# One-pass MLA scores, units by token tile and a folded sample tile in a two-layer encoder step

## Chip, core and metric

The kernel runs on one core of a Trainium2 chip. The metric is the time of one execution on the device in microseconds, as the median of several runs; lower is better.

## The reference, cut to what matters

The kernel computes two layers for a prompt of 512 frames and for 32 new frames of a stream with 128 cached frames ("sample"). All values are fp32, the model width is 1024.

```python
# layer 1, stick-breaking: 16 heads of 64
h = rms_norm(x, g_pre_a)
q, k, v, gate = split(h @ w_in_a, 4);  q, k = rms_norm(q), rms_norm(k)
w = where(mask, exp(log_sigmoid(z) + after), 0)     # after: sums of log_sigmoid(-z) of later keys
x = x + (silu(gate) * (w @ v)) @ w_o_a
# shared latent (512) and rotary key (64) of every frame
latent, kpe = rms_norm(a[:, :512]), rope(rms_norm(a[:, 512:]))      # a = rms_norm(x) @ w_kv_a
k_nope, v = split(latent @ w_kv_b);  k_nope = rms_norm(k_nope)
# layer 2, MLA: 8 heads, 128 + 64 query columns, 128 value columns
qa, gate = split(rms_norm(x) @ w_in_b);  q = rms_norm(qa) @ w_q_b   # then norms and rope
s = (q_nope @ k_nope.T + q_pe @ kpe.T) * 192 ** -0.5
x = x + (silu(gate) * (softmax(where(mask, s, -1e30)) @ v)) @ w_o_b
y = rms_norm(x, g_final)
```

The mask of the prompt is causal, in the MLA layer by chunks of 64 frames.

## The kernel before

**Tiles.** The prompt is four token tiles of 128 (`NT` = 4), the sample a fifth of 32 rows (`TT` = 5), and the cached MLA keys a sixth chunk (`LT` = 6). `TOK` is 544.

**High and low parts.** Large products are not made as fp32 matmuls. ACT copies a value to its high part in a one-pass type (fp32r), DVE or POOL subtracts to get the low part, and TensorE adds three products: high x high, high x low, low x high (`three`, lines 428 to 430). Weights come by SP's DMA queue in pieces of a group into `raw`; ACT makes `whi` (line 1125) and POOL `wlo` (line 1506). A piece is a step "W". Attention scores and value products are true fp32 matmuls, which the profile shows as two records each.

**Orders written out by hand.** Each stage runs steps over pairs of heads. In a step the attention of pair p is mixed with the projections of pair p + 1. A list gives the order, and every engine walks the same list and does its own part of each entry: `STEP_A` and `LAST_A` in the stick-breaking layer (8 pairs), `FILL_D`, `STEP_D` and `LAST_D` in the MLA layer (4 pairs). All queues run in order. Letters of `STEP_A`: C projection chunk of a token tile, G gate, X and Z turns of queries and keys, S scores of a unit, T turn of its weights, O value product. Letters of the MLA lists: Q and K projection chunks (Q queries, K keys and values of two heads), N norm of a chunk, X and Y the turns of a chunk by TensorE into the bank `XB` with ACT's copy to `q2t` or `k2t`, P the last such turn of the pair, S scores of a unit with DVE's maximum (line 1999) and ACT's exponential (line 1429), R its scaling by DVE (line 2007), T the turn of the weights with ACT's copy `wt2`, O the value product and gate. In `LAST_D` H is the split of one head's gated result, E and F are k-steps of the first two of ten output products (`last_product`).

**A chunk in the MLA layer.** TensorE makes it, ACT squares it (and copies the values of a K chunk), DVE sums and forms the mean, POOL raises it to -1/2 (line 1663), DVE makes the norm (and the rotation of a Q chunk), TensorE turns it, ACT copies it.

**A unit** is one head and one query tile against its 1 to 4 key tiles; unit 0 is the sample of both heads. In the MLA layer units go head by head, and a head has one value product over all tiles in the bank `OUT` (line 1023), so O has three parts: sample and two heads.

**Sample tile.** Its stationary operand is 128 columns wide like the others, of which 32 are the sample; the rest of the output rows is not used. It costs three products like the others.

The main MLA list before begins:

```python
STEP_D = [("Q", 0), ("P", 5), ("N", 0), ("K", 0), ("S", 0), ("N", 1), ("R", 0), ("Q", 1), ("X", 0), ("S", 1),
          ("N", 2), ("Y", 0), ("R", 1), ("T", 0), ("K", 1), ("S", 2), ("N", 3), ("W", 0), ("R", 2), ("O", 0),
          ("T", 1), ("Q", 2), ("S", 3), ("X", 1), ("N", 4), ("R", 3), ("K", 2), ("Y", 1), ("Q", 3), ("T", 2),
```

## Time and profile before

| what | value |
|---|---|
| median of 3 runs | 852.7 us (851.94 to 853.42) |
| the profiled execution, its own time | 846.55 us |
| its span, first to last instruction | 844.7 us |
| granted TensorE clock, mean | 0.991 |
| TensorE matmuls busy | 800.8 us, 95% of the span |
| DVE, ACT, POOL busy | 451.9, 331.0, 314.6 us |

The profile is of one execution, which took 6.2 us less than the median of the runs. Durations below come from it. A matmul's record is longer than its share of the engine, since matmuls overlap; the distance from start to start is what it costs. PE is TensorE, PEld its weight loads, DVE VectorE, ACT ScalarE, POOL GpSimd. The stages are: start and first projections to 60 us, eight stick-breaking steps to 394, output product and residual to 460, latent and query projections and gates to 570, the MLA fill to 602, three MLA steps to 759, the last one to 792, output products to 838, tail.

### The profile page before, as it was taken

The numbers are of one execution on the slowest core, as the hardware profiler recorded it, in microseconds if no ns is written. First come the engines' busy times: TensorE is split into PE (matmuls) and PEld (weight loads), VectorE is DVE, ScalarE is ACT, GpSimd is POOL, SyncE is SP. The second block draws the span as 40 slices with busy tenths as digits, with TensorE's granted clock in tenths as the row PEclk, the third lists the DMA queues.
The fourth block names the chain that finished last, engine by engine and source line by source line (L and its number), as shares of the span: only waits on it lengthen the run. The fifth ranks groups of instructions, "written<-read, shape, count | busy, mean of one in ns | idle before, by whom it ended". The sixth has DMA issues, their size and how long they took to land.

```text
span 844.7 us, 13543 instructions
## 1 busy us (share of the span) xinstructions
PE 800.8 (95%) x4623; PEld 654.1 (77%) x4623; DVE 451.9 (53%) x1023; ACT 331.0 (39%) x840; POOL 314.6 (37%) x261
## 2 busy tenths in 40 slices
PE   5799999999999999988999899999999999999996
PEld 4688888878887878756878878998777777765785
DVE  5556666666767585874146432116755555656222
ACT  6444334333333333442177332324444343446211
POOL 5345252534344343551313453445433233333100
PEclk9899999999999999999999999999999999999999
DMA  7631303030303030313223142321102011020211
GB/s 212 159 102 47 87 29 106 26 109 25 107 25 107 25 107 25 101 47 113 79 87 111 69 146 75 88 88 45 44 23 66 1 41 59 26 96 5 106 50 57
DMA packets 68082, 61.68 MB, mean 73 GB/s; under 512 B 7144, under 2 KB 55040, under 8 KB 68032
## 3 DMA queue, kind: packets, MB, share of 16 engines
q1 hardware_dynamic: 68032, 61.04, 23.6%
q8 instruction: 29, 0.48, 0.3%
q14 instruction: 21, 0.17, 0.1%
HBM read 50.85 MB, written 10.17 MB: 72 GB/s over the span
## 4 chain that ended last, share of the span: by engine, by line
PE 87%; DVE 5%; ACT 3%; SPq 1%; issue 1%; POOL 1%; DMA 1%; POOLq 0%; ACTq 0%; DVEq 0%
PE bank L428 17%; PE bank L430 16%; PE bank L429 16%; PE bank L688 5%; PE bank L722 3%; PE bank L995 3%; PE bank L700 3%; PE bank L1039 2%; PE bank L1041 2%; PE bank L1040 2%; PE bank L1023 2%; PE bank L993 2%; PE bank L758 2%; PE bank L760 2%; PE bank L759 2%; PE bank L972 1%
## 5 line engine op out<-in xcount | busy, mean ns | idle before, releaser
L1506 POOL TENSOR_TENSOR wlo<-raw,whi 128x1024 fp32r<-128x1024 f32 (+3 forms) x80 | 194.8, 2443 | 116.8 <-ACT whi L1125 116.5
L428 PE MATMUL bank<-whi,hthi 128*128 128x384 f32 (+1 forms) x360 | 129.5, 360 | 2.5 <-DVE wlo L1717 2.3
L430 PE MATMUL bank<-whi,htlo 128*128 128x384 f32 (+1 forms) x360 | 126.1, 350 | 0.0
L429 PE MATMUL bank<-wlo,hthi 128*128 128x384 f32 (+1 forms) x360 | 126.0, 350 | 0.0
L1125 ACT ACTIVATE whi<-raw 128x1024 fp32r<-128x1024 f32 (+3 forms) x84 | 82.4, 1007 | 24.8 <-PE bank L760 20.6
L1780 DVE TENSOR_TENSOR_SCAN left<-stay 128x512 f32<-128x512 f32 (+4 forms) x72 | 70.8, 983 | 18.8 <-ACT stay L1217 18.5
L1569 POOL TENSOR_TENSOR rstd<-msq,neg_half 128x4 f32<-128x4 f32 x40 | 40.3, 1007 | 98.4 <-DVE msq L1747 97.6
L428 PE MATMUL bank<-hthi,whi 128*128 128x272 f32 x256 | 75.0, 293 | 0.0
L428 PEld LDWEIGHTS bank<-whi,hthi 128*128 128x128 f32 x360 | 69.7, 194 | 6.6 <-issue 5.1
L430 PE MATMUL bank<-hthi,wlo 128*128 128x272 f32 x256 | 73.6, 287 | 0.0
L429 PE MATMUL bank<-htlo,whi 128*128 128x272 f32 x256 | 73.4, 287 | 0.0
L1663 POOL TENSOR_TENSOR rstd<-msq,neg_half 128x2 f32<-128x2 f32 (+1 forms) x44 | 36.8, 837 | 97.7 <-DVE msq L1946 97.3
L430 PEld LDWEIGHTS bank<-whi,htlo 128*128 128x128 f32 x360 | 69.4, 193 | 1.7
L429 PEld LDWEIGHTS bank<-wlo,hthi 128*128 128x128 f32 x360 | 69.5, 193 | 1.5
L1785 DVE TENSOR_TENSOR wgt<-left 128x512 f32<-128x512 f32 (+4 forms) x72 | 66.1, 918 | 3.0
L1182 ACT ACTIVATE sq<-bank 128x256 f32<-128x256 f32 x40 | 15.4, 386 | 112.2 <-PE bank L430 112.2
L688 PE MATMUL bank<-qkt 64*128 64x512 f32 (+3 forms) x128 | 51.4, 482 | 0.0
L429 PEld LDWEIGHTS bank<-htlo,whi 128*128 128x128 f32 x256 | 48.3, 189 | 0.0
L428 PEld LDWEIGHTS bank<-hthi,whi 128*128 128x128 f32 x256 | 48.3, 188 | 0.0
L430 PEld LDWEIGHTS bank<-hthi,wlo 128*128 128x128 f32 x256 | 48.2, 188 | 0.0
L1574 POOL TENSOR_TENSOR gtlo<-gated,gthi 128x544 f32 (+1 forms) x8 | 10.8, 1355 | 94.0 <-ACT gthi L1244 94.0
L1217 ACT ACTIVATE stay<-bank 128x512 f32<-128x512 f32 (+4 forms) x72 | 30.2, 420 | 30.5 <-PE bank L690 29.4
(202 smaller groups left out, 1749.4 us busy)
## 6 DMA issues: line engine op xcount, KB each, us to landing
raw<-in_w_in_a SPq DMA_DIRECT2D x64, 256.0 KB, 3.1
raw<-in_w_in_b SPq DMA_DIRECT2D x24, 256.0 KB, 3.2
raw<-in_w_o_a SPq DMA_DIRECT2D x16, 256.0 KB, 2.8
raw<-in_w_kv_b SPq DMA_DIRECT2D x16, 256.0 KB, 3.1
raw<-in_w_o_b SPq DMA_DIRECT2D x16, 256.0 KB, 3.1
raw<-in_w_q_b SPq DMA_DIRECT2D x16, 192.0 KB, 2.4
x_in<-in_x_prompt SPq DMA_DIRECT2D x4, 512.0 KB, 5.2
out<-qkn SPq DMA_DIRECT2D x8, 256.0 KB, 2.4
```

The source lines that it names most:

```text
L428: eng.matmul(dst, st[0], mv[0], start=(k == 0), stop=False)
L429: eng.matmul(dst, st[0], mv[1], start=False, stop=False)
L430: mm = eng.matmul(dst, st[1], mv[0], start=False, stop=(k == n - 1))
L688: pe.matmul(b[:, 0:(i + 1) * P], qkt[r, par, 0, i * P:(i + 1) * P], qkt[r, par, 1, 0:(i + 1) * P], start=True, stop=True)
L700: mm = pe.transpose(TRB[ub][:, j * P:(j + 1) * P], wgt[:, ub, j * P:(j + 1) * P], ident[:, :])
L1125: nc.scalar.activation(whi[slot][:, c], raw[:, c], ACT.Copy).then_inc(s_hi, 1)
L1217: nc.scalar.activation(stay[0:r, ub, SEQ - n:SEQ], SCR[ub][0:r, 0:n], ACT.Sigmoid, scale=-1.0).then_inc(s_stay, 1)
L1506: nc.gpsimd.tensor_tensor(wlo[slot][:, c], raw[:, c], whi[slot][:, c].bitcast(F32), ALU.subtract).then_inc(s_lo, 1)
L1569: nc.gpsimd.tensor_tensor(rstd[:, sl, :], msq[:, sl, :], neg_half[:, :], ALU.pow).then_inc(s_rs, 1)
L1663: nc.gpsimd.tensor_tensor(rstd[:, sl, 0:w], msq[:, sl, 0:w], neg_half[:, 0:w], ALU.pow).then_inc(s_rs2, 1)
L1780: v.tensor_tensor_scan(out=left[0:r, ub, SEQ - n:SEQ][:, ::-1], data0=back, data1=back, initial=1.0, op0=ALU.mult, op1=ALU.bypass).then_in ...
L1785: v.tensor_tensor(wgt[0:r, ub, 0:n], left[0:r, ub, SEQ - n + 1:SEQ + 1], left[0:r, ub, SEQ - n:SEQ], ALU.subtract).then_inc(s_wgt, 1)
```

## The change

1. **Scores of the MLA layer.** Queries and keys are split like the projections: `qh`, `ql`, `kh`, `kl`, `kpeh`, `kpel`. The rotary part of a query is stacked: 64 rows of its high part on 64 rows of its low part (`qr`), against the rotary key, which lies in both halves. A prompt unit is then five one-pass products in place of two fp32 ones. Keys are padded to 256 columns. ACT copies a turned Q chunk in two operations, DVE subtracts the low parts from `XB` (three operations for Q, one for K). The next turn waits for them (`s_xlo2`).
2. **Units by token tile.** `UNIT_D` takes both heads of a tile one after the other. A value product is per tile and head, of 128 columns each, so O has five parts. There is one query buffer in place of two.
3. **Orders.** Chunks go K0 K1 Q3 K2 Q2 K3 Q1, sample K and Q, cached K, Q0. `FILL_D`, `STEP_D` and `LAST_D` are rewritten: C is a chunk, V its turn with ACT's copy and DVE's low part.
4. **Folded sample.** The low part of the sample lies in 32 more columns of the high part, so that one stationary operand holds both. Two products in place of three give both halves in different rows, which are added afterwards: in `STEP_A` by a copy of ACT and an addition of DVE (step L), in the two output products by a second addition. POOL fills the columns.
5. **Last products.** Order of tiles 3, 2, 1, 0, sample; three products are begun inside the last step (E, F, B); the last two heads are split tile by tile (J).
6. **Stick-breaking.** The weights are written over `stay`; the tile `wgt` is gone.

```diff
-UNIT_D = [None] + [(h, i) for h in range(2) for i in reversed(range(NT))]
+UNIT_D = [None] + [(h, i) for i in reversed(range(NT)) for h in range(2)]
+CHUNKS = [("K", 0), ("K", 1), ("Q", 3), ("K", 2), ("Q", 2), ("K", 3), ("Q", 1), ("K", NT), ("Q", NT), ("K", TT), ("Q", 0)]
+STEP_D = [("C", 0), ("P", CD - 1), ("S", 0), ("N", 0), ("C", 1), ("R", 0), ("S", 1), ("N", 1), ("V", 0), ("C", 2),
+          ("T", 0), ("R", 1), ("N", 2), ("V", 1), ("S", 2), ("W", 0),
+          ("C", 3), ("O", 0), ("T", 1), ("R", 2), ("N", 3), ("S", 3), ("V", 2), ("C", 4), ("T", 2), ("R", 3), ("N", 4),
+          ("V", 3), ("S", 4), ("O", 1), ("W", 1),
+          ("C", 5), ("T", 3), ("R", 4), ("N", 5), ("S", 5), ("V", 4), ("C", 6), ("T", 4), ("R", 5), ("N", 6), ("V", 5),
+          ("S", 6), ("O", 2), ("W", 2),
+          ("C", 7), ("T", 5), ("R", 6), ("N", 7), ("S", 7), ("V", 6), ("C", 8), ("T", 6), ("R", 7), ("N", 8), ("V", 7),
+          ("S", 8), ("O", 3), ("W", 3),
+          ("C", 9), ("T", 7), ("R", 8), ("N", 9), ("V", 8), ("C", 10), ("T", 8), ("N", 10), ("V", 9), ("O", 4)]
 FILL_D = []
...
+    FILL_D.append(("C", _j))
     if _j:
         FILL_D.append(("N", _j - 1))
     if _j in (2, 4, 6, 8):
         FILL_D.append(("W", (_j - 2) // 2))
     if _j > 2:
-        FILL_D.append((TURN[CHUNKS[_j - 3][0]], CHUNKS[_j - 3][1]))
+        FILL_D.append(("V", _j - 3))
+LAST_D = [("P", CD - 1), ("S", 0), ("H", 0), ("S", 1), ("R", 0), ("H", 1), ("W", 0), ("E", 0), ("T", 0), ("R", 1), ("S", 2),
+          ("H", 2), ("E", 1), ("O", 0), ("T", 1), ("R", 2), ("S", 3), ("W", 1), ("E", 2), ("H", 3), ("T", 2), ("R", 3),
+          ("S", 4), ("E", 3), ("O", 1), ("F", 0), ("H", 4), ("T", 3), ("R", 4), ("S", 5), ("W", 2), ("E", 4), ("H", 5),
...
 # proj_a, TensorE
+                if c == NT:
+                    two(pe, b[:, 0:3 * P], [(acol(ht[0], k, c, HS), w[k]) for k in range(KD)]).then_inc(s_proj, 1)
+                    return
 # turn_qk, TensorE
                 if begun(CD * q + c):
                     pe.wait_ge(s_xev2, CD * q + c)
+                if begun(LD * q + lows(c)):
+                    pe.wait_ge(s_xlo2, LD * q + lows(c))
 # score_d, TensorE
-                pe.matmul(b[:, 0:(i + 1) * P], q2t[:, par, h, i * P:(i + 1) * P], k2t[:, par, h, 0:(i + 1) * P], ...)
-                pe.matmul(b[:, 0:(i + 1) * P], q2t[r, par, 2, i * P:(i + 1) * P], kpet[r, 0:(i + 1) * P], ...)
+                n = max(2, i + 1) * P
+                pe.matmul(dst, qh[:, h, tile], kh[:, par, h, 0:n], start=True, stop=False)
+                pe.matmul(dst, qh[:, h, tile], kl[:, par, h, 0:n], start=False, stop=False)
+                pe.matmul(dst, ql[:, h, tile], kh[:, par, h, 0:n], start=False, stop=False)
+                pe.matmul(dst, qr[:, h, tile], kpeh[:, 0:n], start=False, stop=False)
+                pe.matmul(dst, qr[:, h, tile], kpel[:, 0:n], start=False, stop=True)
 # out_d, TensorE
+                for h in range(2):
+                    for j in range(i + 1):
+                        mm = pe.matmul(OUT[:, c0 + h * P:c0 + (h + 1) * P], v2[:, par, h, j, :], wt2[:, h, j, :], ...)
 # xlo_d, DVE, new
+                if what == "K":
+                    v.tensor_tensor(kl[:, par, :, tile], nope, kh[:, par, :, tile].bitcast(F32), ALU.subtract).then_inc(s_xlo2, 1)
+                    return
+                v.tensor_tensor(ql[:, :, tile], nope, qh[:, :, tile].bitcast(F32), ALU.subtract)
+                for h in range(2):
+                    last = v.tensor_tensor(qr[other, h, tile], XB[own, 2 * P:3 * P], qr[own, h, tile].bitcast(F32), ALU.subtract)
+                last.then_inc(s_xlo2, 1)
```

## Rows read from the trace of the kernel before

**Rows 1.** Page, chain that ended last, share of the span by engine.
```profile
PE 87%; DVE 5%; ACT 3%; SPq 1%; issue 1%; POOL 1%; DMA 1%; POOLq 0%; ACTq 0%; DVEq 0%
```

**Rows 2.** Windows: length, busy PE PEld DVE ACT POOL (records), clock, DMA share, GB/s.
```profile
276.70:319.90 43.20, 42.91 (x282) 35.86 (x282) 28.65 (x45) 16.37 (x41) 17.98 (x10) 1.00 0.21 64
...
570.20:602.02 31.82, 30.34 (x159) 26.41 (x158) 23.09 (x79) 13.05 (x31) 17.83 (x16) 1.00 0.20 59
602.02:654.32 52.30, 51.79 (x255) 38.17 (x255) 28.91 (x110) 22.82 (x61) 17.66 (x15) 1.00 0.13 36
...
758.94:792.36 33.42, 32.21 (x139) 19.38 (x138) 16.94 (x37) 16.63 (x39) 9.72 (x6) 1.00 0.20 75
792.36:838.30 45.94, 45.90 (x198) 36.85 (x197) 11.11 (x14) 5.26 (x9) 2.98 (x8) 1.00 0.10 40
```

**Rows 3.** Timeline of PE in a stick-breaking step: start, us, what.
```profile
283.69 0.34 PE L428 MATMUL bank<-whi,hthi 128*128 128x384 f32 x1
...
291.37 0.34 PE L430 MATMUL bank<-whi,htlo 128*128 128x384 f32 x1
...
308.98 0.29 PE L428 MATMUL bank<-hthi,whi 128*128 128x272 f32 x1
...
311.45 0.28 PE L430 MATMUL bank<-hthi,wlo 128*128 128x272 f32 x1
```

**Rows 4.** Chain in the first MLA step: start, us on the chain, what.
```profile
611.39 0.86 PE bank L993 x2
612.25 1.05 PE bank L995 x2
613.46 0.23 PE bank L972 x2
...
614.14 0.23 PE bank L429
...
618.31 0.33 PE bank L1018 x2
...
629.19 0.22 PE bank L993 x2
629.42 0.41 PE bank L995 x2
...
637.37 2.21 PE bank L1023 x8
```

**Rows 5.** Timeline of DVE in the second MLA step.
```profile
660.48 0.29 DVE L1988 TENSOR_TENSOR qn<-pe_tmp 128x128 f32<-128x128 f32 x1
...
665.69 0.69 DVE L1999 TENSOR_REDUCE neg_max<-bank 128x1 f32<-128x512 f32 x1 [0.93 <-PE bank L997]
...
683.48 0.29 DVE L2007 TENSOR_SCALAR prob<-prob,p_inv 128x128 f32<-128x128 f32 x1
...
689.65 0.61 DVE L1962 SCALAR_TENSOR_TENSOR kn<-bank,rstd,g_kn 128x128 f32<-128x128 f32 x2 [0.81 <-POOL rstd L1663]
...
702.42 0.61 DVE L2007 TENSOR_SCALAR prob<-prob,p_inv 128x128 f32<-128x128 f32 x1
```

**Rows 6.** Timeline of ACT in the second MLA step.
```profile
656.45 0.49 ACT L1398 ACTIVATE sqd<-bank 128x384 f32<-128x384 f32 x1 [4.04 <-PE bank L430]
...
666.42 0.69 ACT L1429 ACTIVATE prob<-bank,neg_max 128x512 f32<-128x512 f32 x1 [2.26 <-DVE neg_max L1999]
...
671.71 0.94 ACT L1125 ACTIVATE whi<-raw 128x896 fp32r<-128x896 f32 x1
...
676.76 0.48 ACT L1414 ACTIVATE q2t<-bank 128x384 f32<-128x384 f32 x1
...
687.73 0.38 ACT L1401 ACTIVATE sqd<-bank 128x256 f32<-128x256 f32 x1 [1.21 <-PE bank L430]
```

**Rows 7.** Timeline of POOL in the fill ahead of the MLA steps.
```profile
579.82 2.12 POOL L1506 TENSOR_TENSOR wlo<-raw,whi 128x896 fp32r<-128x896 f32 x1
```

**Rows 8.** Timeline of DVE before the fill, a gate's product with PSUM.
```profile
564.78 0.44 DVE L1919 TENSOR_TENSOR sg<-bank,sigc 128x272 f32<-128x272 f32 x1 [2.57 <-ACT sigc L1381]
```

More of the change, by code:

```diff
@@ L430, in three, with two @@
                 mm = eng.matmul(dst, st[1], mv[0], start=False, stop=(k == n - 1))
+            return mm
+        def two(eng, dst, pairs):
+            n = len(pairs)
+            for k, (st, mv) in enumerate(pairs):
+                eng.matmul(dst, st, mv[0], start=(k == 0), stop=False)
+                mm = eng.matmul(dst, st, mv[1], start=False, stop=(k == n - 1))
             return mm
@@ L1667, in step_d @@
                 for what, n in order_d(p):
[L1668 to L1669 removed]
+                    if what == "C" and ahead:
+                        rms_d(p + 1, 1 - par, *CHUNKS[n])
                     elif what == "W":
@@ L1955, in norm_d @@
                 dve.wait_ge(s_act2, CD * q + c + 1)
-                before = CD * q + (CHUNK_D[what, t - 2] + 1 if t > 1 else 0)
+                rank = RANK_D[what, t]
+                before = CD * q + max([0] + [CHUNK_D[s] + 1 for s in CHUNKS if s[0] == what and RANK_D[s] == rank - 2])
                 if begun(before):
```

535 lines of the change are left out of this document (333 added, 202 removed), and 18 rows, old and new, of tables (LAST_D, STEP_A, STEP_D).

## The prediction

> **What bounds the kernel now.** I read the chain that ended last first: TensorE carries 87% of it [rows 1]. Then the busy time by stage, to see how full TensorE is where the change works [rows 2]. In a stick-breaking step 42.9 of 43.2 us are busy. The fill ahead of the MLA loop takes 31.8 us, a full MLA step 52.3 (three of them, 602.0 to 758.9), the last step 33.4 and the output products 45.9. Every matmul taken out there gives its whole period back, as long as the others keep up. Whether they do is read from the third view, the timelines of the other engines [rows 5 to 8]: what a chunk or a unit takes from TensorE's result until TensorE can use it again. All queues are in order, so a late piece holds up everything written behind it.
>
> **TensorE's own work.** The price of a high/low matmul comes from starts: 45 of 384 columns begin between 283.69 and 291.37 us, 0.175 us each; 21 of 272 columns between 308.98 and 311.45, 0.124 each [rows 3]; one of 512 takes 0.23 [rows 4].
>
> *Folded sample.* A pair's sample chunk drops from 24 to 16 matmuls: 8 pairs x 8 x 0.175 = -11.2 us. The new ACT copy and DVE add lie behind four other chunks' worth of work before the transposes need them, and DVE is busy 28.7 of 43.2 us [rows 2]; if that cover were gone it would cost about 1 us a pair. In the first output product 8 of 512 columns go in each half, 16 in all, but six of them in the last stick-breaking step, where TensorE waits for DVE anyway; 10 x 0.23 = -2.3. POOL's extra 32 columns there lie on the path: +0.3. The second product loses 16: -3.7.
>
> *Scores.* A 512-key unit costs 0.86 + 1.05 us for its two fp32 products and 0.16 for the mask, 2.07 in all; the 128-key one 0.22 + 0.41 + 0.16 [rows 4]. Five one-pass products cost 5 x 0.23 = 1.15, 5 x 0.175, and 5 x 0.12 for 256 and for 128 keys (padded to 256; 256 columns lie just under the 272-column row). With 0.07 for a mask that no longer follows a 64-row product: 1.22, 0.94, 0.66, 0.66 against 2.07, 1.65, 1.22, 0.80. A head saves 2.26, a pair 4.5, four pairs -18. With the mask's 0.16 kept it is -15.
>
> *Value products.* A head's 4 products, 1280 columns in all, become 10 of 128. They take 2.21 us now [rows 4]. An fp32 matmul of 128 columns takes 0.22 (both records), so 10 take 2.2: nothing. The other bound is the 32-column product of the sample, which took 0.33 for its two records: +1.1 a head, +8.8 in all. I take nothing, since the row of 0.22 has the new shape, 128 columns on 128.
>
> *Edits I cost at nothing.* The sigmoid of unit u in the stick-breaking layer now waits for the turn of unit u-2, and not its scan; TensorE does that turn ahead of the score the sigmoid needs, so the wait is always met. Copies into the single query buffer wait for scores of the tile that stand several entries ahead in STEP_D. SP loads the residual in another order and `g_final` behind it, after the last score, where some 35 us of output products lie ahead of the first norm; without that cover it would be a few us once. The five banks for the last products take away waits that TensorE does not have now (45.9 of 45.9 us busy) [rows 2].
>
> By TensorE alone the sum is -11.2 - 2.0 - 3.7 - 18 = -35 us.
>
> **What the new order does to the others.** This is the part that decides. Three things come together. XB is one bank: chunk c+1 may be turned only when the low part of chunk c is subtracted by DVE (`s_xlo2`), which stands behind ACT's copies. In STEP_D a chunk's norm N now stands ahead of the next unit's S, so DVE takes the maximum only after it. And ACT's weight piece W stands behind that unit's exponential, with POOL's piece ahead of the next chunk's power.
>
> Prices [rows 5 to 8]: a Q chunk from its square to the end of its norm 656.45 to 660.77, 4.3 us; a K chunk 687.73 to 690.26, 2.5, of it 0.8 waiting for POOL and 0.6 norm, so 1.3 once POOL is free; maximum 0.7 for 512 keys, taken as 0.5 and 0.35 for fewer; exponential 0.69 and the read of its sum, 0.8, taken as 0.7 and 0.6 for fewer; ACT's piece 0.94; POOL's piece 2.12. Q evacuation was one 0.48 copy, now two, 0.66. The low part is 0.4 for K (a 272-column operation on PSUM took 0.44) and 0.8 for Q, that plus two 128-column ones.
>
> Walk one step, C0 at 0. Chunks cost 2.75 (K) and 2.1 (Q). C0, turn, S0, C1, S1, turn, C2: chunk 2 (Q) ends at 10.9. Then norm 4.35, low part K 0.4, maximum 0.6, exponential 0.8, ACT piece 0.95, POOL piece 2.15, power and norm of chunk 3 1.3, maximum 0.5, exponential 0.7, Q copies 0.65, low part Q 0.8: about 13 us, until 23.9. TensorE has 10 us of its own work in between (V1, S2, C3, O0, T1, S3, V2, C4, T2: 20.5), and its next turn V3 waits 2.9 with its score, O1 and chunk 5 queued behind. From that low part the loop closes again: sums 0.8, power 1.0, norm 1.65, low 0.4, maximum 0.5, exponential 0.65, pieces 0.9 + 2.15, power and norm 1.3, maximum 0.35, exponential 0.6, copies 0.65, low 0.8 = 11.8, against 9.4 of TensorE's work: V5 waits 2.5. V5 to V7 is 11.2 against 8.5: 2.7. V9 needs chunk 9's norm, 8.7 against 7.1: 1.6. A step has 46.6 us of TensorE's work and takes 56.4; before it had 51 and took 52.3. Three steps: +12.3.
>
> *Fill.* Two chunks, K and Q, are 5.4 us of TensorE's work. DVE and POOL in series take sums 0.85, power 1.0, POOL piece 2.12, Q norm 1.65, Q low part 0.85 = 6.5. Walked from the first chunk, V1, V3, V5, V7 and V9 wait 1.5, 1.3, 1.2, 1.2 and 0.6, 5.8 us in all, where before 1.5 was lost at the end: +4.3.
>
> *Last step and products.* The turn of the last chunk (Q0) is no longer covered by a K chunk: 2.9. E, F and B stand right behind the H that feeds them. H's DVE part stands behind a maximum, and its ACT part behind a weight piece: E0 waits 1, T1 2, E2 1.3, E3 2, the rest 1.5, 7.7 in all. From the step's start to the last product: 2.9 + 33.6 of work + 7.7 + 35.1 of products left = 79.3, the same as 758.94 to 838.28 now. The 8 us saved there are eaten.
>
> The lock of an SBUF port bears on this: a DVE scale of 128 columns took 0.61 us while POOL's piece ran (702.42), against 0.29 for the same operation at 683.48 [rows 5]. The Trainium skill's page "SBUF — State Buffer", section "Who interferes with whom", says that DVE's two-port modes, and DVE operations with two SBUF inputs, wait for a reading POOL operation to end; the trace agrees with the 0.61. By that rule R1 and R3 of the last step wait for the piece (my T1 above, from the row); the low parts, with one input in PSUM, would not.
>
> *Shared latent.* Four low parts of the rotary key go ahead of latl on DVE, 0.2 to 0.5 each, mostly in stretches that wait on DVE: +0.8. *Tail.* The sample tile needs two more half additions, one exposed: +0.7.
>
> **Sum.** -11.2 - 2.0 + 0.8 + 4.3 + 12.3 + 0 + 0.7 = +4.9 us. The profiled execution took 846.55 us (span 844.7 and 1.9 around it), so it would become 851.4. The median of the runs lies 6.2 above it, 852.7, and I put the change on that: about 857.5.
>
> **Rivals.** The first two end on the other side. *The others keep up* (TensorE stays the bound): -35, and +1.5 for latent and tail, 819. Speaks for it: DVE is busy only 29 of 52 us in a step, ACT 22, POOL 18 [rows 2]. Against: those are sums, and the chain above is a wait, not a load. 0.12. *POOL's piece is not in the loop* (ACT reaches its piece earlier, or raw and order let the power go ahead): three waits a step lose 2.1 each, 3 x 6.3 = -19: 838. It decides once the loop is below 10 us. 0.20. *The value products pay for their weight loads* at 0.33 a product: 866; 0.07. *The loops are longer still* (handoffs of 0.1 in twelve links, or R in the way of N): 868; 0.05. The forecast itself, waits as walked, 850 to 865: 0.56.
>
> What a measurement of this kernel tells from no change is 0.2%, 1.7 us. Of the forecast 0.10 lies within it, the rest above. Faster 0.32, within 0.11, slower 0.57. Range: down to 836 to take in the second rival, up to 868 for the value bound; outside are the first rival and a little above.
>
> **What would show it.** Right: about 41.8 us for a stick-breaking step; an MLA step of 54 to 58 with TensorE idle before the transposes of kn at V3, V5 and V7, released by DVE's subtraction from XB; a fill of about 36; POOL's piece starting later after its chunk than now. Wrong: steps near 47 to 50 without such gaps, an L1023 successor over 0.12 us a record, or a sample fold that holds up the transposes of a pair. The forecast fails first where the order of S, N and W on DVE and ACT binds less than I walked it.

## The result, and the profile after

The changed kernel took 896.4 us in the median of four runs, the kernel before 852.3 beside it: a ratio of 1.0505, 95% interval 1.0454 to 1.0555. It is 44 us slower. I had forecast slower, but 857.5 and at most 868.

First the page of the changed kernel: busy time by engine, and the chain that ended last by engine.

```profile
PE 799.3 (90%) x4655; PEld 668.5 (75%) x4655; DVE 485.6 (55%) x1121; ACT 336.5 (38%) x867; POOL 313.9 (35%) x270
...
PE 52%; issue 15%; DVE 15%; POOL 10%; ACT 5%; SPq 1%; DMA 1%; POOLq 0%; DVEq 0%; ACTq 0%
```

TensorE carried 87% of the chain before [rows 1] and carries 52% now. VectorE, POOL and ScalarE together went from 9% to 30%, and "issue", time in which an engine waited for nothing that the profile shows, from 1% to 15%.

Then the stages: a stick-breaking step, the fill, two MLA steps, and the last step with the output products. The columns are those of [rows 2], and the rows answer to them.

```profile
283.57:326.93 43.36, 42.01 (x274) 34.84 (x275) 28.89 (x46) 16.75 (x42) 18.29 (x11) 1.00 0.21 64
577.95:615.90 37.95, 31.15 (x158) 26.02 (x157) 22.90 (x87) 13.73 (x34) 17.82 (x16) 1.00 0.17 49
615.90:676.84 60.94, 53.20 (x286) 44.55 (x286) 36.04 (x125) 23.35 (x65) 16.66 (x14) 0.92 0.11 31
676.84:738.21 61.37, 53.53 (x288) 44.66 (x287) 36.73 (x128) 21.79 (x63) 17.67 (x15) 0.92 0.10 32
800.20:883.40 83.20, 74.43 (x354) 58.98 (x353) 34.39 (x76) 22.61 (x52) 13.87 (x15) 0.96 0.14 53
```

Two things are to be seen. An MLA step leaves TensorE idle for 7.8 of 61.4 us, and its granted clock in that step is 0.92 of full speed, where it was 1.00 [rows 2]. Over the whole span it was 0.959 against 0.991 before. The stages add up as follows (us, from one profiled execution of each; the last column is my sum cut to the same stages).

| stage | before | after | change | forecast |
|---|---|---|---|---|
| start to the first stick-breaking step | 60.3 | 62.7 | +2.4 | -1.4 |
| seven steps | 303.1 | 308.4 | +5.3 | -9.8 |
| last stick-breaking step to the fill | 206.9 | 206.9 | 0 | -1.2 |
| fill | 31.8 | 38.0 | +6.1 | +4.3 |
| three MLA steps | 156.9 | 184.3 | +27.4 | +12.3 |
| last step and output products | 79.3 | 83.1 | +3.8 | 0 |
| tail | 6.4 | 7.2 | +0.8 | +0.7 |
| sum | 844.7 | 890.5 | +45.8 | +4.9 |

**The MLA step.** The waits of TensorE in the second one, grouped by what it waited for, and then the chain across the wait ahead of V3 (start, us on the chain, what).

```profile
PE bank L1049 <- DVE qr L2163: 7.3, 3, 2.9
PE bank L1110 <- ACT wt L1568: 0.3, 1, 0.3
```

```profile
695.90 0.43 DVE ssq L2097
...
696.36 1.47 DVE msq L2100
...
697.89 0.71 POOL rstd L1798
...
698.62 0.61 DVE kn L2117 x2
699.23 0.47 DVE neg_max L2175
...
700.40 0.27 ACT qh L1540
700.67 0.28 ACT qr L1541
...
700.98 0.41 DVE ql L2158
...
702.16 0.63 PE bank L1049 x2
```

This is the loop that I walked, link by link: chunk, mean square, POOL's power, norm, maximum, exponential, copies, low part, turn. The three waits stand at V3, V5 and V7, released by the last subtraction from XB. POOL's piece shows in it twice: the power starts at 697.89, right behind the piece (695.67 to 697.79), and the mean square of 2 columns took 1.47 us while the piece ran, where the next one took 0.17. The maximum, and the exponential behind it, are in this loop because of the new order.

What I did not see coming is behind the wait. Here are the transposes at its end and a score product behind them, and the same product of 512 keys at full clock.

```profile
702.16 0.63 PE L1049 MATMUL bank<-ident,kn 128*128 128x128 f32 x2 [2.92 <-DVE qr L2163]
...
702.90 0.52 PE L1076 MATMUL bank<-kl,qh 128*128 128x384 f32 x1
703.22 0.52 PE L1077 MATMUL bank<-kh,ql 128*128 128x384 f32 x1
...
714.97 0.41 PE L1049 MATMUL bank<-ident,kn 128*128 128x128 f32 x2 [1.49 <-DVE qr L2163]
```

```profile
623.62 0.40 PE L1075 MATMUL bank<-kh,qh 128*128 128x512 f32 x1
623.86 0.40 PE L1076 MATMUL bank<-kl,qh 128*128 128x512 f32 x1
```

At 702.9 a product of 384 columns starts 0.32 us before the next; at 623.6 one of 512 starts 0.24 before it. From 702.2 to 705.6 the granted clock is at its lower level, 1.2 GHz (0.5), and again from 726.1 to 732.9, at V7's wait. Each of the three MLA steps of this trace has 10.2 us at 1.2 GHz, and each such stretch begins near the end of an idle one of 2.9 us (from 1.3 us ahead of its end to 0.1 behind it). The kernel before had none in its MLA layer.

**The stick-breaking step.** The folded sample chunk takes 2.98 us in place of 4.36, as forecast. But the step takes 43.2 to 44.2 us at full clock, not 41.8, and one of the seven, with 6.8 us at 1.2 GHz, takes 46.2. TensorE's waits over the seven steps:

```profile
PE bank L770 <- DVE stay L1925: 7.9, 10, 1.1
...
```

These are the turns T2 (3.0 us in four of the steps) and T3 (4.9 in six). VectorE and POOL around them, in the second step:

```profile
123.99 3.47 DVE L1922 TENSOR_TENSOR_SCAN left<-stay 128x512 f32<-128x512 f32 x1
127.49 2.66 DVE L1925 TENSOR_TENSOR stay<-left 128x512 f32<-128x512 f32 x1
...
132.80 0.95 DVE L1922 TENSOR_TENSOR_SCAN left<-stay 128x384 f32<-128x384 f32 x1
133.78 2.55 DVE L1925 TENSOR_TENSOR stay<-left 128x384 f32<-128x384 f32 x1
136.25 0.94 DVE L1922 TENSOR_TENSOR_SCAN left<-stay 128x384 f32<-128x384 f32 x1
137.23 0.56 DVE L1925 TENSOR_TENSOR stay<-left 128x384 f32<-128x384 f32 x1
```

```profile
123.97 5.63 POOL L1633 TENSOR_TENSOR wlo<-raw,whi 128x1024 fp32r<-128x1024 f32 x2 [0.90 <-ACT whi L1226]
...
133.42 2.49 POOL L1633 TENSOR_TENSOR wlo<-raw,whi 128x1024 fp32r<-128x1024 f32 x1 [1.65 <-ACT whi L1226]
```

One subtraction of the same shape took 0.56 us and, beside POOL's piece, 2.55. T3 waits for it. Before, it was as long:

```profile
217.42 2.56 DVE L1785 TENSOR_TENSOR wgt<-left 128x384 f32<-128x384 f32 x1
```

It ended at 219.98 and T3 started at 220.19 without a wait: the sample chunk's longer work stood there and covered it, by 0.2 us.

### The profile page after: what moved, and what is told of

It is laid out like the page before. It is cut to its first block, busy times and chain, and to the rows that moved or that the text cites. A ratio compares the mean times of both kernels' runs of the same rounds, so it can differ in the third digit from the quotient of the medians.

```text
span 890.5 us, 13800 instructions
## 1 busy us (share of the span) xinstructions
PE 799.3 (90%) x4655; PEld 668.5 (75%) x4655; DVE 485.6 (55%) x1121; ACT 336.5 (38%) x867; POOL 313.9 (35%) x270
## 4 chain that ended last, share of the span: by engine, by line
PE 52%; issue 15%; DVE 15%; POOL 10%; ACT 5%; SPq 1%; DMA 1%; POOLq 0%; DVEq 0%; ACTq 0%
PE bank L485 9%; PE bank L487 9%; PE bank L486 9%; POOL wlo L1633 4%; POOL rstd L1696 3%; PE bank L1110 2%; PE bank L1133 2%; PE bank L1134 2%; DVE left L1922 2%; PE bank L757 2%; PE bank L828 2%; PE bank L792 2%; PE bank L829 2%; PE bank L1136 2%; PE bank L770 1%
## 5 line engine op out<-in xcount | busy, mean ns | idle before, releaser
L1633 POOL TENSOR_TENSOR wlo<-raw,whi 128x1024 fp32r<-128x1024 f32 (+3 forms) x80 | 190.6, 2390 | 162.3 <-ACT whi L1226 162.2
L485 PE MATMUL bank<-whi,hthi 128*128 128x384 f32 (+1 forms) x296 | 107.8, 364 | 2.7 <-DVE wlo L1852 2.1
L487 PE MATMUL bank<-whi,htlo 128*128 128x384 f32 (+1 forms) x296 | 104.9, 354 | 0.0
L486 PE MATMUL bank<-wlo,hthi 128*128 128x384 f32 (+1 forms) x296 | 104.0, 351 | 0.0
L1922 DVE TENSOR_TENSOR_SCAN left<-stay 128x512 f32<-128x512 f32 (+4 forms) x72 | 74.7, 1038 | 20.0 <-ACT stay L1327 19.4
L486 PE MATMUL bank<-htlo,whi 128*128 128x272 f32 x256 | 74.4, 291 | 0.0
L1925 DVE TENSOR_TENSOR stay<-left 128x512 f32<-128x512 f32 (+4 forms) x72 | 68.7, 954 | 2.5
L485 PEld LDWEIGHTS bank<-whi,hthi 128*128 128x128 f32 x296 | 57.6, 195 | 6.9 <-issue 5.4
L486 PEld LDWEIGHTS bank<-wlo,hthi 128*128 128x128 f32 x296 | 57.5, 194 | 1.4
L487 PEld LDWEIGHTS bank<-whi,htlo 128*128 128x128 f32 x296 | 57.1, 193 | 1.7
L1550 ACT ACTIVATE prob<-bank,neg_max 128x512 f32<-128x512 f32 (+4 forms) x36 | 18.4, 512 | 88.8 <-DVE neg_max L2175 88.6
```

Of the source, the lines that this page charges most:

```text
L485: eng.matmul(dst, st[0], mv[0], start=(k == 0), stop=False)
L486: eng.matmul(dst, st[0], mv[1], start=False, stop=False)
L487: mm = eng.matmul(dst, st[1], mv[0], start=False, stop=(k == n - 1))
L1550: nc.scalar.activation(prob[0:r, ub, 0:n], SCR[ub][0:r, 0:n], ACT.Exp, bias=neg_max[0:r, ub:ub + 1], accum_out=p_sum[0:r, ub:ub + 1]).then ...
L1633: nc.gpsimd.tensor_tensor(wlo[slot][:, c], raw[:, c], whi[slot][:, c].bitcast(F32), ALU.subtract).then_inc(s_lo, 1)
L1922: v.tensor_tensor_scan(out=left[0:r, ub, SEQ - n:SEQ][:, ::-1], data0=back, data1=back, initial=1.0, op0=ALU.mult, op1=ALU.bypass).then_in ...
```

## The experiments

All comparisons are ratios to the kernel before, run in turn with it on the same chip.

**1. Fillers in the waits.** In STEP_D and LAST_D an entry D ahead of V3, V7 and P:

```
+ pe.wait_ge(s_expd, UA * p + n - 1)
+ for _ in range(20):
+     pe.transpose(SCR[(par + n) % 2][:, 0:P], ident[:, :], ident[:, :])
```

> The changed kernel with one addition: before the turns V3 and V7 of each MLA step and before P of the last step TensorE makes 20 transposes of the identity into the score bank that is free then, 20 x 0.109 = 2.2 us, in a wait that took 2.9 us in the changed kernel. No result uses them. Theory A (the drop of the granted clock to 0.5 follows these idle stretches): TensorE no longer stands still for 2.9 us there, the granted clock stays at 1.0, a step goes from 61.3 us to 56.3 (10.2 us a step ran at 0.5), and the kernel gains 3 x 5.1 + 1.7 = 17 us: 879. Rival B (the clock falls for another reason, such as the long stretches of mixed work ahead): the rows at 0.5 stay, and the time stays at 896. Rival C (the fillers themselves hold up the turns): some us slower than 896.

Measured: 1.0499 (1.0463 to 1.0535). The second MLA step, and its waits:

```profile
682.20:741.05 58.85, 54.77 (x329) 46.61 (x327) 37.33 (x129) 21.93 (x64) 17.69 (x15) 0.97 0.08 26
```

```profile
PE bank L1050 <- DVE qr L2169: 3.3, 2, 2.6
```

Where TensorE was kept at work, the clock stayed: no stretch at 1.2 GHz follows V3, V7 or P. One of 3.4 us stands at V5 in two of the three steps; its wait grew from 1.5 us to 2.6 and, in the third step, 2.9. But the clock costs less than its face value: the second step went from 61.4 to 58.9 us, not to 56.3. TensorE at half speed between V3 and V5 works while VectorE walks the next round of the loop; at full speed it arrives earlier and waits longer. The three steps of this trace are 4.9 us shorter. The whole kernel shows nothing of it: the interval is 3 us each way, and this execution took 6.4 us more outside these steps, 4.5 of them between the stick-breaking steps and the fill, where its trace has 30.7 us at 1.2 GHz (one stretch of 17.1 at 376) and that of the changed kernel 13.6.

Other traces add to this. The changed kernel's own and those of runs 3, 4, 5, 8 and 10, which leave the MLA stage as it is, have 33 waits of 2.9 us at V3 and V7, and 30 of them have a stretch at 1.2 GHz that begins near their end; the six waits that the fillers cut to 0.73 us or less have none. So the lower clock goes with the idle stretch, but not without exception. The three exceptions are V3 of the second step in runs 4, 5 and 10. There V5 waited 2.6 us, one stretch of 3.4 us stands at it, and the step took 58.9 us: what the fillers gave, without a filler. And in the third step of these runs the waits at V3, V5 and V7 are those of the changed kernel (2.9, 1.5, 2.9) with 6.8 us at 1.2 GHz in place of 10.2; it took 60.9 us in place of 62.0, so that 3.4 us at the lower clock cost 1.1.

**2. Weight pieces behind the norms.** Four edits of this kind in STEP_D:

```
- ("V", 1), ("S", 2), ("W", 0), ("C", 3), ("O", 0), ("T", 1), ("R", 2), ("N", 3), ("S", 3), ("V", 2)
+ ("V", 1), ("S", 2), ("C", 3), ("O", 0), ("T", 1), ("R", 2), ("N", 3), ("W", 0), ("S", 3), ("V", 2)
```

> The changed kernel with the four weight pieces W of STEP_D moved from ahead of chunks 3, 5, 7 and 9 to behind the norms of those chunks, ahead of the next maximum. Theory A (POOL's piece of 2.12 us and ACT's of 0.94 stand in the loop of chunk, norm, maximum, exponential, copies, low part): V3 and V7 lose about 2.2 of their 2.9 us and V5 its 1.5, 5.9 a step; and as no idle stretch of 2.9 us is left, the clock comes back too, 5.1 a step: 3 x 11 = 33 us, 863. Rival B (the pieces only fill time in which DVE waits for TensorE's score anyway): V3 and V7 stay at 2.9 and the kernel at 896. Rival C (the piece now delays the maximum through the port that POOL and VectorE share): the maximum takes over 1 us in place of 0.68, gain below 10 us.

Measured: 1.0283 (1.0245 to 1.0322), 2.2% below the changed kernel's ratio, where A's 33 us are 3.9%. The second MLA step, and TensorE's waits over three steps:

```profile
672.11:725.43 53.32, 48.78 (x288) 40.85 (x287) 34.17 (x128) 21.96 (x63) 17.58 (x16) 1.00 0.09 30
```

```profile
PE bank L1049 <- DVE qr L2163: 12.1, 9, 1.5
```

A step lost 8.1 us: 3.3 of waits, and 4.8 of TensorE's busy time, which is the clock alone, since the work is the same. V3 waits 1.06, V5 1.50, V7 1.47. From V3 to V5 it is 11.2 us in place of 12.8: the round is 1.6 us shorter and the wait in it the same, now with a TensorE at full clock.

**3 and 4. W3 one chunk later; the fold taken out.** In STEP_A `("W", 3)` moves from ahead of `("L", 4)` to behind `("C", 4)`; in the other run the call of `two` for chunk NT and the return behind it are left out, so that `three` is called.

> The changed kernel with the last weight piece W3 of STEP_A moved from ahead of the sample chunk to behind it. In the changed kernel the sample chunk is 1.38 us shorter (4.36 to 2.98), but O1 ahead of T3 grew from 1.02 to 2.19 us: T3 waits for VectorE's subtraction of 2.55 us, which runs beside POOL's W3, against 0.56 without. Theory A: with W3 later that subtraction takes 0.6, T3 does not wait, and a stick-breaking step goes from 43.4 to about 42.1: 7 steps, -9 us, 887. Rival B (the delay comes from POOL's power and the scan before it, W1 and W2): the step keeps its 43.4, and the time stays. Rival C (the lock moves to unit 5 and T5 waits in its place): less than 4 us gained.

> The changed kernel with the sample chunk back at 24 matmuls (three high/low products, the low one on the tile's 32 low columns as before), with the fold's copy and add left in; the sample rows are then summed with a part counted twice, so the sample output differs. Theory A (the fold's saving of 1.38 us a pair is lost at T3, where TensorE waits for VectorE): the wait before T3 takes up the added 1.4 us, a step stays within 0.3 us of 43.4, and the kernel stays within 3 us of 896. Rival B (TensorE is the bound and the fold does save): 8 x 1.4 = 11 us slower, 907.

Measured: 1.0591 (1.0552 to 1.0631) and 1.0568 (1.0539 to 1.0598). W3 later did not help: T3 no longer waits, but W3 now meets unit 5, and T5 and T6 wait 0.35 and 0.39 us (rival C); T2's 0.75 stays, in all six later steps, and the steps without a lower clock are 43.8 to 44.1 long. Unfolded, the steps are 43.4 to 44.7 us, where the changed kernel with its 1.4 us less of matmuls has 43.2 to 44.2 at full clock. TensorE's waits of that run over seven steps:

```profile
PE bank L768 <- DVE stay L1923: 3.7, 5, 0.8
```

Of 7.9 us in waits T3's 4.9 are gone. What is left is T2's, in five steps of this trace (3.7) and in four of the changed kernel's (3.0). The seven steps took 308.8 us, all at full clock; the changed kernel's took 308.4, of them one of 46.2 with 6.8 us at the lower clock. Leave these 2.9 us out and the fold saves it 3.3 us over seven steps, where TensorE does 9.7 less. Neither theory holds whole: in the changed kernel's order the fold keeps a third of its saving. The time of the kernel as a whole (1.0568 against 1.0505) does not decide it: the two intervals touch.

**5 and 8. All pieces of a stick-breaking step earlier, with and without the fold.**

```
+ ("W", 0), ("T", 0), ("W", 1), ("C", 1), ("W", 2), ("C", 2), ... ("T", 4), ("W", 3), ("G", 0)
```

> The changed kernel with all four weight pieces of a stick-breaking step moved: W1 ahead of chunk 1, W2 ahead of chunk 2, W3 ahead of the first gate (the first fill keeps its order). In the changed kernel POOL's W1 and W2 run together for 5.6 to 6.2 us just as VectorE scans unit 2 (3.47 us in place of 1.22 where the piece began first), and W3 beside unit 3's subtraction (2.55 in place of 0.56); T2 waits 0.75 and T3 0.63 us, or T3 1.1. Theory A (these stretches hold VectorE, and VectorE sets when T2 and T3 may go): both waits vanish and the fold's 1.38 us shows, 42.0 us a step in place of 43.4 to 44.2, 7 steps, 12 us less: 2.6% to 3.7% slower than the kernel before in place of 5%. Rival B (another chain, scores to sigmoid to scan, sets them): steps stay at 43.4 and the time stays. Rival C (the pieces' new place holds up chunks 1 and 2 through POOL's power): gain below 4 us.

> The run with the early pieces of the stick-breaking steps, and in it the sample chunk back at 24 matmuls (the fold's copy and add left in, so that the sample rows count a part twice). Theory A (the fold saves TensorE 1.38 us a pair as soon as VectorE does not hold up T2 and T3): 11 us slower than the run with the early pieces, a step at 43.4 in place of 42.0. Rival B (the step is bound by others even then): within 3 us of it.

Measured: 1.0524 (1.0495 to 1.0553) and 1.0633 (1.0595 to 1.0671). T2 and T3 no longer wait, but W3 now meets unit 5, and T5 and T6 wait 0.52 and 0.39: rival C. Most steps are 43.4 to 43.9 and 44.8 to 45.2 us; the seven took 307.5 and 317.4, each with two stretches of 3.4 us at the lower clock. In this order the fold is worth 1.4 us a step, all that TensorE saves by it, and the whole kernel was 1.1% slower without it, as theory A of the eighth run had it. Whether the fold pays is decided by where the weight pieces run.

**6 and 12. Turns ahead of norms and units, with the pieces moved and with them where the change has them.** From chunk 2 on, in the pattern

```
- ("C", 4), ("T", 2), ("R", 3), ("N", 4), ("V", 3), ("S", 4)
+ ("C", 4), ("T", 2), ("R", 3), ("V", 3), ("N", 4), ("S", 4)
- ("C", 5), ("T", 3), ("R", 4), ("N", 5), ("S", 5), ("V", 4)
+ ("C", 5), ("T", 3), ("R", 4), ("V", 4), ("N", 5), ("W", 1), ("S", 5)
```

> The changed kernel with STEP_D in another order: from chunk 2 on the turn V of a chunk stands ahead of the next chunk's norm N and of the next unit's score and maximum S, the weight pieces stand behind the norms as in the second experiment, and O3 stands ahead of chunk 10. Theory A (what V3, V5 and V7 wait for is the loop of norm, maximum, exponential, copies, low part; each link taken out of it shortens it): copies and low part follow a turn at once, about 2.2 us, against 3.9 us of TensorE's own work between two turns; the waits of 1.06, 1.50 and 1.47 us left in the second experiment shrink below 0.3 each, a step goes from 53.3 to about 49.8, and the kernel is 3 x 3.5 = 10 us below the second experiment, 1.6% above the kernel before. Rival B (VectorE's and POOL's own work with its handoffs bounds the step): it stays at 53. Rival C (the turns now come too early for the norms of the query chunks, 4.3 us from square to end): V2, V4 and V6 wait in place of V3, V5 and V7, and the step stays at 53 or over.

> The changed kernel with the turns V ahead of the norms and units as in the sixth experiment, but with the weight pieces W where the change has them (behind S2, S4, S6 and S8). The pieces alone took a step from 61.3 to 53.3 us, both edits together to 50.7. Theory A (the pieces are in the loop only because copies and low part stand behind them; with the turns first the loop is copies and low part alone): a step at 51 to 52, and the kernel within 4 us of the sixth experiment, 2.3% to 2.6% above the kernel before. Rival B (the pieces hold VectorE and POOL's power whatever stands around them): waits of over 1 us stay at V3, V5 and V7, 54 to 56 a step, 3.3% above.

Measured: 1.0212 (1.0165 to 1.0260) and 1.0359 (1.0295 to 1.0423). The second MLA step of the sixth run and its waits over three steps; then the same of the twelfth.

```profile
668.73:719.48 50.75, 48.76 (x288) 41.15 (x287) 34.13 (x128) 21.68 (x63) 17.64 (x16) 1.00 0.10 31
```

```profile
PE bank L1110 <- ACT wt L1568: 3.0, 6, 0.5
PE bank L1049 <- DVE qn L2143: 2.3, 3, 0.8
```

```profile
679.80:736.32 56.52, 49.84 (x289) 41.00 (x287) 38.78 (x129) 21.34 (x64) 17.72 (x15) 1.00 0.09 27
```

```profile
PE bank L1049 <- DVE kn L2117: 9.8, 11, 1.1
```

With both edits V3, V5 and V7 wait for nothing, and a step takes 50.7 us, 1.5 below the kernel before. With the turns alone it takes 56.5: the turns V3, V5, V7 and V9 now wait 0.7 to 1.1 us each for the norm of a key chunk. Ahead of V3 of the second step that norm starts at 702.04, behind the low part of chunk 2, which is subtracted when the piece is over (700.99), and behind POOL's power, which starts at 700.43, right at the piece's end. Theory A of the twelfth run fell, and its rival B has it nearly right. Of the 10.6 us that both edits win a step, the turns alone win 4.9, the pieces alone 8.1.

**7. All orders.** STEP_A of the fifth run and STEP_D of the sixth, `V` ahead of `N` in the fill, and in LAST_D `("H", 0)` ahead of P, each later H a place earlier, and E0 between S0 and S1.

> The changed kernel with the orders of the two runs before it together, in the fill the turn's low part ahead of the norm, and in the last step H0 ahead of P, each later H one place earlier, and E0 ahead of S1. Theory A (all of the 44 us are waits that the orders make; TensorE has 35 us less to do than before): A -12, MLA steps -34 against the changed kernel, fill -3, last step -5 (its wait of 3.6 us ahead of E3 goes): 896 - 54 = 842, 1.2% below the kernel before. Rival B (some of the chains are VectorE's own work): 855 to 865. Rival C (the last step keeps its waits, since the weight pieces still slow the low parts): 5 us more than A.

Measured: 1.0113 (1.0071 to 1.0155), 1.1% above the kernel before where A gave 1.2% below. The fill fell from 38.0 to 36.3 us, the last step and its products from 83.1 to 79.0. The seven stick-breaking steps gained 4 us where A had 12, and 2.9 of these 4 are the changed kernel's stretch at the lower clock; the MLA steps gained 32 where it had 34.

**9 and 10. Pieces in the shadow of chunks 0 to 2; and two covers.** STEP_A in both:

```
+ [("S", 0), ("W", 0), ("C", 0), ("S", 1), ("T", 0), ("W", 1), ("C", 1), ("W", 2), ("C", 2), ("W", 3), ("S", 2), ...
```

and in the ninth, on top of the seventh, before the output products and in the last step:

```
+ EARLY_A = [KD - 2, KD - 1, KD - 1]
...
+ for k in range(EARLY_A[2]):
+     oa_product(2, k)
  for i in range(TT):
      residual(i, 0)
...
+ PEN_D = STEP_D[:-4] + [("T", 8), ("H", 0), ("V", 9), ("N", 10), ("O", 4)]
+ LAST_D = [("E", 0), ("H", 1), ("P", CD - 1), ("S", 0), ("E", 1), ("H", 2), ("S", 1), ...
```

> The run with all orders, and on top of it: in a stick-breaking step the four weight pieces in the shadow of chunks 0 to 2 (W0 ahead of chunk 0, W1 ahead of chunk 1, W2 and W3 around chunk 2); ahead of the first output products that need the last pair, the third product's seven earlier parts, 21 x 0.23 = 4.8 us, in a wait of 2.8 us; and ahead of P in the last step the product E0, whose head is scaled and split in the step before, 0.7 us, with E1 between S0 and S1. Theory A (these are waits with nothing else behind them): T5 and T6 wait no more (0.9 us a step, 6.5 in all), the 2.8 us wait and the 3.4 us at a granted clock of 0.5 behind it go (4.5), P waits 2.5 in place of 3.3, so about 11 us below the run with all orders: 846, level with the kernel before (0.998). Rival B (pieces that early hold up chunk 0's norm and unit 1's scan, and their turns X0 and T1 then wait): steps at 43.4, 852. Rival C (the granted clock falls elsewhere in their place, as it differs from one execution to the next): 849 with a wide interval.

> The changed kernel with only the stick-breaking order of the run beside it. Theory A (VectorE is no longer held by POOL's pieces while units 2 to 6 are scanned): no wait over 0.2 us before T2 to T6, a step at 42.3 us in place of 43.4 to 44.2, so 7 x 1.4 = 10 us below the changed kernel, 3.9% above the kernel before in place of 5.0. Rival B (other chains take its place, as T5 and T6 did with W3 ahead of the gate): 43.2 to 43.4 a step, 4.8% above.

Measured: 0.9865 (0.9822 to 0.9908) and 1.0355 (1.0310 to 1.0400). A stick-breaking step of the tenth run, and two of POOL's pieces in another one:

```profile
315.38:357.32 41.94, 41.81 (x278) 34.72 (x275) 26.74 (x46) 16.54 (x42) 16.62 (x11) 1.00 0.20 63
```

```profile
245.30 2.37 POOL L1636 TENSOR_TENSOR wlo<-raw,whi 128x1024 fp32r<-128x1024 f32 x1
...
249.54 2.40 POOL L1636 TENSOR_TENSOR wlo<-raw,whi 128x1024 fp32r<-128x1024 f32 x1
254.70 1.01 POOL L1699 TENSOR_TENSOR rstd<-msq,neg_half 128x4 f32<-128x4 f32 x1 [2.76 <-DVE msq L1885]
```

All four pieces are done by 252 us, 21 us into the step, before unit 3 is scanned. No turn waits, TensorE is busy 41.8 of 41.9 us, and the step is the 41.8 that I had forecast for the change itself. The seven steps are 14.4 us shorter than the changed kernel's. The ninth run is the first version faster than the kernel before, by 1.4%; its A had given 0.2%. Its trace is 11.6 us shorter than that of the seventh run, as A had it, while the ratio moved by 21 us; what makes up the rest isn't in the two traces. It changes three things over the seventh run, and beside the stick-breaking order (run 10) no run separates them.

**11, 14 and 15. The same edits on the kernel before, and a control.** The eleventh and the fourteenth are one kernel: STEP_A of the kernel before with W0 to W3 in the shadow of chunks 0 to 2, and the third output product's early parts. The fifteenth is the kernel before unchanged.

> The kernel before (not the changed one) with the two edits outside the MLA layer that the best run has: the four weight pieces of a stick-breaking step in the shadow of chunks 0 to 2, and the third output product's seven earlier parts ahead of the products that need the last pair. Theory A (the fold is what these pieces set free: before, TensorE was busy 42.9 of 43.2 us in a step, so nothing can be gained there): steps stay at 43.2, only the 2.57 us wait goes, and the kernel gains 2 to 4 us, 0.3% to 0.5%. Rival B (the order by itself is worth as much on the kernel before, and the change has no part in the best run's gain): steps fall to about 42 too, 12 us or 1.4% faster.

> The kernel before with the two edits outside the MLA layer, once more, beside the best run's successor and the plain kernel before. Theory A (the last comparison overstated it, since the stages of its trace add up to 4.4 us): 0.993 to 0.996, and the changed kernel in its best order is 0.5% to 1% faster than it. Rival B (the two are level): 0.986, and the changed kernel's 16 us less of TensorE work are given back in full by fill, steps and start.

> The kernel before, unchanged, as a control with a trace of its own. Theory A: ratio 1.000 within 0.3%, stages as in the trace of before (steps of 43.2 and 52.2 us, granted clock at 0.5 in four short stretches). Rival B (the kernel before has more of the lower clock in some executions, and the one traced first had little): ratio still 1.000, but more stretches at 0.5 and a span some us over 844.7; that would explain why e11's measured gain exceeds the 4.4 us of its trace.

Measured: 0.9862 (0.9815 to 0.9909), 0.9893 (0.9863 to 0.9924), and 0.9984 (0.9958 to 1.0010) for the control. The kernel before gains over 1% by two edits that have nothing of the change, more than the 4.4 us by which the stages of its trace fell: the time is rival B's of run 11, though a step does not fall to 42 (43.0 to 43.4). The control's trace has part of the rest: its seven steps took 308.6 us, those of the trace that I predicted from 303.1. Two of its steps, and VectorE's scan of unit 2 and POOL's piece in the first of them:

```profile
191.28:238.35 47.07, 46.11 (x283) 38.22 (x283) 29.11 (x45) 16.52 (x41) 17.16 (x10) 0.93 0.20 59
...
281.88:325.96 44.08, 43.12 (x283) 35.93 (x283) 29.09 (x45) 16.54 (x41) 16.97 (x10) 1.00 0.20 63
```

```profile
209.28 3.48 DVE L1780 TENSOR_TENSOR_SCAN left<-stay 128x512 f32<-128x512 f32 x1
```

```profile
209.26 2.42 POOL L1506 TENSOR_TENSOR wlo<-raw,whi 128x1024 fp32r<-128x1024 f32 x1 [0.90 <-ACT whi L1125]
```

In the trace that I predicted from, the same scan took 1.22 us and POOL's piece beside it 3.41:

```profile
121.36 1.22 DVE L1780 TENSOR_TENSOR_SCAN left<-stay 128x512 f32<-128x512 f32 x1
```

```profile
121.34 3.41 POOL L1506 TENSOR_TENSOR wlo<-raw,whi 128x1024 fp32r<-128x1024 f32 x1 [0.91 <-ACT whi L1125]
```

The two start within 0.02 us of each other. Whichever gets ahead holds the other up: the scan loses 2.3 us, or the piece 1. In all the traces, where a piece started 0.04 us or more behind such a scan the scan took 1.2 us, and where it started 0.05 to 0.5 ahead 3.4; at 0.02 ahead both are seen. Of the control's seven steps three lose it at T2 (0.8 us of TensorE each, 2.5 in all), and next to one of these waits the clock fell for 6.8 us. So the kernel before has a coin toss in six of its seven steps (in the first the piece starts 0.15 us behind the scan), and one profiled execution shows only how it fell. The coin is not even: in the two traces of the kernel before the scan lost in 3 of 12 such steps, in the seven of the changed kernel that keep its stick-breaking order of W1 and W2 in 33 of 42. With the pieces moved there is nothing to toss for unit 2: all its steps took 43.0 to 43.4.

**13. The first pair not folded.** On top of the ninth: `three` for chunk NT of the first pair, and no copy and add there.

```
- if c == NT:
+ if c == NT and not (isinstance(q, int) and q == 0):
```

> The best run of the changed kernel, with the first pair's sample chunk (the one in the fill of the stick-breaking layer) not folded: three products, 24 matmuls, no copy and no add; the seven other pairs keep the fold. In the changed kernel the second gate of that fill waits 2.53 us for this chunk's longer chain (copy, add, square, sums, power, scale), and the granted clock is at 0.5 for 3.4 us behind it. Theory A (in the fill the chain is not covered): 1.4 us more of matmuls, 1.3 to 2.5 us less of waiting, and up to 1.7 less at the lower clock; the first step starts 1 to 3 us earlier than its 63.9, about 0.2% faster than the best run: 0.984. Rival B (the fill is bound by the loads of x and its rows before the gates): start within 0.5 us of 63.9.

Measured: 0.9829 (0.9798 to 0.9859), 835.7 us, the best of all. Its first step starts at 60.8 us in place of 63.9. In the changed kernel that was this wait, with VectorE's scale of the folded chunk as its end:

```profile
56.47 0.36 PE L485 MATMUL bank<-hthi,whi 128*128 128x272 f32 x1 [2.53 <-DVE qkr L1896]
```

Run in turn with it, the kernel before with its two edits took 841.0. The change as a whole, in its best order, is worth 5.3 us or 0.6% over it. No run looks for a better order of the MLA layer in the kernel before, so this is not what the change would be worth with both at their best.

## Why the prediction was right and wrong

**Right: direction and the mechanism of the MLA waits.** The turns at V3, V5 and V7 wait for the low part out of the one bank XB, in the chain as walked, and P waits for the norm of its own chunk, which nothing covers. I had 2.9, 2.5, 2.7 and 2.9 us; the trace has 2.92, 1.49, 2.91 and 2.88. That V3's 2.9 is met to the digit is luck: the links as I listed them add up to 13.2 us and not 13, and with TensorE's 10 they leave 3.2. The value products cost nothing: 10 products of 128 columns start 0.112 us apart a record, as before (0.109), and that rival is out. The five-pass score of 512 keys takes 1.17 us and its mask 0.06, where I had 1.22 in all. The first output product and the latent came out within 1.2 us together, the tail within 0.1. Of the signs that I had named, the idle time before V3, V5 and V7 and its releaser came; the stick-breaking step of 41.8, the MLA step of 54 to 58 and the fill of 36 did not (43.2 to 44.2, 61 and 38).

**Wrong: the size, in three terms.** The largest is the MLA step, where the sum had no term for TensorE's lower clock; the second is the fold, whose saving of 11.2 us did not come.

*Three MLA steps, forecast +12.3, measured +27.4.* A step of 61.4 us is 48.8 of TensorE's work at full clock (the busy time of the sixth run), 4.8 more for the clock, and 7.8 idle. I had 46.6 and 9.7. So the work was 2.2 too low. One part is the base, for which I took 51 where the row says 51.8 [rows 2]. The other is the saving, 3.0 and not 4.4 by that row: from start to start in the second step the eight prompt units with their masks took 11.6 us before and take 7.8 (run 6), where I had 7.0, since the first of the five products costs 0.04 to 0.09 more than the others, and the turns of the weights take 0.5 more. The waits were 1.9 too high. V5's and V9's shrink behind a slow TensorE: where the clock did not fall at V3 (runs 4, 5 and 10, second step), V5 waits 2.6 as walked and V9 0.7. And the clock was not in the sum at all, 4.8 us a step: that is the step that failed most. I had costed an idle stretch as what it lasts; here 2.9 us were followed by slowed work. The Trainium skill states the rule in "TensorE: Matmul & The Clock Gate", section "HAM oscillation — how this bites in real kernels": a kernel whose TensorE waits again and again pays, on top of the waits, half of the time spent at the lower clock. By it 10.2 us at 1.2 GHz are 5.1, an estimate by that section; the busy time shows 4.8, so the trace agrees on the work. It does not agree on the step: with 6.8 us less of it a step won 2.5, not 3.4, since part of the slow work lies beside the wait that comes next (run 1, and the second steps of runs 4, 5 and 10).

*Folded sample, forecast -11.2, measured +7.7 to the last of the seven steps, the start included.* The step that failed is "Every matmul taken out there gives its whole period back, as long as the others keep up". That they do was taken from VectorE's 28.7 of 43.2 us busy and from the cover of the new copy and add alone. The copy and the add were indeed covered in the steps. What was not covered is what the longer chunk itself had covered: unit 3's subtraction, which runs beside POOL's piece and ends 0.6 to 1.1 us after TensorE is ready for T3. Seven steps were to be 9.7 us shorter and were 5.3 longer. Of these 15 us 4.9 are T3's waits (gone in run 4), and 3.0 are waits at T2, which run 4 keeps without the fold (the toss of run 15). One stretch at the lower clock has 2.9, and the unchanged chunks, which took 0.2 us a step longer, 1.4; some 3 us are spread over rows too small to name. With the pieces out of the way the fold's whole saving shows (runs 5 and 8, and run 10 with 41.9 us a step). In the first fill the chain of the folded chunk has no units to hide behind, 2.5 us at the second gate (run 13).

*Last step and products, forecast 0, measured +3.8.* The waits were 8.8 us, 10.6 forecast, and the busy time 74.4, 68.7 forecast; 6.8 us at 1.2 GHz explain some 3.4 of these 5.7, and the rest is work that I had too low. Half of the largest wait, 3.6 us ahead of E3, is in this pair of rows of VectorE and POOL:

```profile
818.02 2.42 DVE L2198 TENSOR_TENSOR glo<-sg,ghi 128x544 fp32r<-128x544 f32 x1 [2.23 <-ACT ghi L1574]
```

```profile
817.52 2.34 POOL L1633 TENSOR_TENSOR wlo<-raw,whi 128x1024 fp32r<-128x1024 f32 x1 [3.61 <-ACT whi L1226]
```

The same subtraction took 0.72 us where POOL was idle (810.26), so 1.7 of the 3.6 us are the piece's. The Trainium skill's rule from "SBUF — State Buffer", section "Who interferes with whom", which I had weighed for R1 and R3 alone, covers it: a VectorE operation with two SBUF inputs waits while POOL reads. By that rule each of the scans, subtractions and H's beside a piece had to be priced at the piece's end. The low parts out of XB have one input in PSUM. In the changed kernel none of them ran beside a piece; in run 2 five did and took the same 0.42 us, so there the trace of run 2 agrees too. Of the rest of E3's wait another 1 us lies ahead of the subtraction: ScalarE's high part `ghi` stood behind ScalarE's own part of the weight piece, 1.05 us from 816.40.

**The fill**, +6.1 against +4.3: its waits were 6.8 us, 5.8 forecast, and before there were 1.5.

**Rivals.** "Others keep up" (819) did not hold; the same work in another order comes within 17 us of it, 835.7. "POOL's piece is not in the loop" did not hold for the change as made; made true by an edit it was worth 19 us (1.0505 to 1.0283). That its own sum says 19 as well is luck: a step lost 3.3 us of waits, not 6.3, and 4.8 by the clock. "Loops longer" had the right sign and no cause for the size.

**What stays open.** Why the granted clock falls behind some of the shorter idle stretches (0.8 us in the control, 0.75 in the changed kernel at 261.7) and not behind others of the same length, and why it did not fall behind 3 of the 33 of 2.9 us. Why executions differ so much in the time at 1.2 GHz between the stick-breaking steps and the fill (13.6 us in the changed kernel's trace, 30.7 in that of run 1). And why the changed kernel's scan loses the toss more often.

## What to carry to other kernels

Before taking work off the engine that sets the pace, ask what that very work covers, at its place: the wait behind it appears at the next hand-over, and a share of busy time over a whole step does not show it. Place bulk work of POOL where VectorE has nothing with two SBUF inputs to do; here the same four pieces in another place were worth 14 us over seven steps to the changed kernel, and 1 to 7 to the kernel before, by how its toss had fallen. And price idle stretches of TensorE like the 2.9 us here at more than their length, but check what waits behind them: slowed work beside a wait costs less than half of its time (2.5 us for 6.8 here).

## What the runs showed of the hardware

- The granted clock of TensorE fell to 1.2 GHz for 3.4 or 6.8 us at a time at 30 of 33 idle stretches of 2.9 us in the MLA steps of six traces, and at none of six where identity transposes filled 2.2 of these 2.9 us (run 1). The kernel before has such stretches too, of different number in different executions: 13.6 us outside the tail in one trace, 34 in the control's.
- Two operations that start 0.02 us apart on VectorE and POOL can fall either way: scan 1.22 and piece 3.41 us, or scan 3.48 and piece 2.42. With POOL 0.05 to 0.5 us ahead it was always the scan that lost, with POOL 0.04 behind always the piece.
- A VectorE operation on two columns (the mean square, SBUF to SBUF with one input) took 1.47 us beside POOL's piece and 0.17 without. A subtraction with one input in PSUM took 0.42 us beside a piece and without one (run 2).
